# Decode step with paged attention: key pages transposed on VectorE in 32x32 blocks, scores in 32x32 tiles of TensorE

## The chip, the cores and the metric

The kernel runs on one core of one Trainium2 chip, in one launch. The metric is the time on the device in microseconds. Before the change three runs took 1260.12, 1259.9 and 1259.26 us (median 1259.9).

## The reference, cut to what matters

One layer of a decoder trunk, all in fp32, for 512 prompt tokens and for 8 sample sequences of 8 new tokens each, with the same weights. Model width is 1024.

```python
h = rms_norm(x) ; qkv = h @ w_in                      # 1024 x 3072, then rotary on q and k
# A) differential attention: 4 heads, two 64-wide components, values 128 wide
oa = (softmax(q1 k1^T) - lam * softmax(q2 k2^T)) v ; oa = rms_norm_per_head(oa) * (1 - lambda_init)
# B) dilated window attention: 8 heads x 64, union of (128,1), (512,4), (2048,16)
x += concat(oa, ob) @ w_out
x += (silu(h2 @ w_gate) * (h2 @ w_up)) @ w_down       # h2 = rms_norm(x), FF = 2816
y = rms_norm(x)
```

The sample sequences look back on 4096 past tokens. For A the keys and values lie in pages of 128 tokens x 512 numbers (256 KB), 32 per sequence, found through a page table. For B they are 2048 rows of 512 numbers per sequence, of which 10 blocks of 128 rows are read. So 336 blocks ("pages") of keys and 336 of values are loaded, 176 MB in all. New keys, values and the shifted windows are outputs as well.

## The kernel before, in words

**Slots.** Two sequences make an item. There are 8 items: 4 for A, of 8 quads each, and 4 for B, of 3 quads each, 44 quads in all (`KSLOTS`). A quad is 4 pages of each of the two sequences (2 of each in the last quad of a B item). The middle of the kernel is a loop over slots `t` and steps `i` = 0..7, written out in the same order on every engine. In slot t the keys of quad t are scored, and the values of quad t - 8 (`LAG`) are weighed. Slots 0 to 7 have keys only, 44 to 51 values only.

**Keys of a slot.** SP loads page (t, i) into `k_ring[i]` once the page that lay there has been read (L563). TensorE turns it with four 128x128 transposes into one of two PSUM banks `TB` (`turn_page`, L988). ACT (even pages, L1374) and VectorE (odd pages, L1686) copy the bank to `kt_sb`, which holds four pages, one half of a slot. After pages 0 to 3, and again after 4 to 7, `score_keys` (L1016) multiplies: for each of 4 heads f, 128 rows of contraction, 32 query rows and 512 keys, into 32 partitions of bank `S`. The query blocks `q_bd` are written by POOL (L741). At the end of the slot VectorE takes the scores out of `S` with mask and running maximum (`keep_scores`, L1711).

**Values of a slot.** Probabilities are transposed through bank `X` (L1028), copied by ACT (L1384) and multiplied with the value pages (L1049).

**Pieces.** Everything of the prompt is cut into 297 pieces that are strung between the steps: 192 of the projection (24 tiles of 8 pieces, each 6 matmuls, L833), 2 for the last transposes, 70 of prompt attention (32 units of 128 queries, two pieces a unit, and 3 units of run-out), 33 of the w_out product (8 tiles of 4, L964, and the last way back, L977). `upto(t, i)` says how many pieces are done by a step: 32 before slot 0, 5 a slot up to slot 6, some 5.3 a slot up to slot 43, and the 33 of w_out over slots 44 to 51. A unit's two score matmuls (L879) go to the banks `M[0]` and `M[1]`, rows 0 to 63 and 64 to 127 of the array; VectorE masks both (L1602). Outputs of prompt attention and transposed tokens use bank `Y`.

**Queues.** SP issues all loads in the order of the loop. Between the pages it puts the weight chunks (512 KB each), window shifts, at slot 44 the four blocks of x (L652 waits for the last unit of prompt attention), and at slot 46 the 4 MB load of w_out into `wo_sb` (L677), which the sample product L1142 needs. Behind the slots come L1142, the second norm, and the FFN (L1114).

Of the kernel before, what the change touches and what calls it, by code (L numbers as in the profile page):

```python
# [15 lines left out]
P = 128  # L16
# [168 lines left out]

def upto(t, i):
    if i < 0:
        t, i = t - 1, 7
    if t < 0:
        return 8 * PRE  # L190
    if t < 7:
        return 8 * PRE + 5 * t + -(-5 * (i + 1) // 8)
    if t < KSLOTS:
        a = 8 * PRE + 35
        return a + -(-(OUT - a) * (8 * (t - 7) + i + 1) // (8 * (KSLOTS - 7)))
    return min(PIECES, OUT + -(-(PIECES - OUT) * (8 * (t - KSLOTS) + i + 1) // (8 * LAG)))
# [19 lines left out]
def x_order():  # L216
    out = []
    for t in range(SLOTS):
        for i in range(8):
# [6 lines left out]
            for p in pieces(t, i):  # L226
                if ATTN <= p < OUT:
# [10 lines left out]
def y_order():  # L238
    out = []
    for p in range(ATTN):  # L240
        n, j = divmod(p, 8)
        if j == 5 and 0 < n < TILES and kind_of(n - 1):
            out.append(("t", n - 1))
        if (n, j) in GROUP_AT:
            out.append(("g", GROUP_AT[n, j]))
        if p == 8 * TILES:
            out.append(("t", TILES - 1))
        if p == 8 * TILES + 1:
            out.append(("g", 3))
    out += [("a", T) for T in range(KT)]  # L250
    return {what: k for k, what in enumerate(out)}


X_NO, Y_NO = x_order(), y_order()
# [44 lines left out]
def build(nc, ins, outs):  # L299
    from contextlib import ExitStack  # L300
    ctx = ExitStack()
    with ctx:
# [13 lines left out]
        small = at("small", [P, 184], region(768))  # L316
# [17 lines left out]
        o_lo = [at("o_lo0", [P, D], W0 + 31744, F32R), at("o_lo1", [P, D], W0 + 4096, F32R)]  # L334
# [7 lines left out]
        qT = at("qT", [P, KT, NT], Q0)  # L342
        kT = at("kT", [P, KT, NT], Q0 + 18432)
# [33 lines left out]
        y_prompt = at("y_prompt", [P, 2, SEQ], KS)  # L377
# [6 lines left out]
        pt_sb = at("pt_sb", [P, 2, 4, P], region(4096))  # L384
        ptm = at("ptm", [NS, P], region(512))
        q_bd = at("q_bd", [P, 2, 2, 4, 32], region(2048))
# [19 lines left out]
        g_max = small[:, 96:105]  # L406
# [42 lines left out]
        x_full, x_free, y_full, y_free = sem("x_full"), sem("x_free"), sem("y_full"), sem("y_free")  # L449
# [6 lines left out]
        qbd_zero, q_ready = sem("qbd_zero"), sem("q_ready")  # L456
        t_done, kt_act, kt_dve = sem("t_done"), sem("kt_act"), sem("kt_dve")
# [45 lines left out]
        def _(sp):  # L503
# [75 lines left out]
            def store_k(n):  # L579

                T = tile_of(n)
                sp.wait_ge(y_free, Y_NO["t", n] + 1)
# [4 lines left out]
            def store_group(g):  # L587

                s, keys = g // 2, g % 2 == 0
                sp.wait_ge(y_free, Y_NO["g", g] + 1)  # L590
# [18 lines left out]
            def main(p):  # L609
# [21 lines left out]
                if p == ATTN + 8:  # L631
                    sp.wait_ge(y_free, Y_NO["g", 3] + 1)
# [15 lines left out]
            for t in range(SLOTS):  # L648
                for i in range(8):
                    h, k = divmod(i, 4)  # L650
                    if has_k(t + 1) and k < pages_of(t + 1):
                        sp.wait_ge(t_done, PAGE_NO[t, i] + 1 if k < pages_of(t) else half_end(t, h))  # L652
                        load_page(True, t + 1, i)
                    for p in pieces(t, i):
                        main(p)
                    if k == 3 and has_v(t + 1) and t < KSLOTS:
                        q = t + 1 - LAG
                        if t == KSLOTS - 1:
                            sp.wait_ge(t_done, half_end(t, h))
# [63 lines left out]
        def _(pool):  # L723
# [7 lines left out]
            def fetch_q(it):  # L731

                if it >= 2:
# [1147 lines left out]
```

## Time and profile before

| | |
|---|---|
| median of 3 runs | 1259.9 us |
| the profiled execution | 1257.03 us |
| its span, first to last instruction | 1255.1 us |
| mean granted TensorE clock | 0.968 of full |
| busy: PE, DVE, ACT, POOL | 88%, 34%, 37%, 20% |
| DMA queue of the loads | 74.2% of 16 engines' span, 314 MB |
| last instruction of the keys' stage | 681.4 us |

The slots lie between 55.9 us (first copy of a page) and 785.1 us (start of L1142). Busy shares are means over the span; a stretch has its own limit, so the table by stretches is the view to read. A matmul's record lasts some 0.27 us although the next one starts much sooner, so records overlap, and one fp32 matmul of 32 columns of weights leaves two records.

### The profile page before, as it was taken

Reading aid. Unit: us, or ns where it says so; the run is one execution under the profiler, and the core shown is the slowest. Engines: PE = TensorE matmul, PEld = TensorE weight load, DVE = VectorE, ACT = ScalarE, POOL = GpSimd, SP = SyncE. Lnnn points to the kernel's source line nnn. Section 1 sums busy time; section 2 is a strip of 40 time slices with the busy share of each in tenths; the row PEclk is TensorE's granted clock in tenths of the full one; section 3 lists DMA queues with packets and bytes.
Section 4 is the critical chain, followed back from the end, with each engine's and each line's share of the span. In section 5 each row is a group of like instructions: output and inputs, shape, how many; then the busy total and the mean of one; then the engine's idle time right before and its main releaser. Section 6 shows DMA issues by size and latency. Waiting matters only on the chain.

```text
span 1255.1 us, 27090 instructions
## 1 busy us (share of the span) xinstructions
PE 1108.4 (88%) x10450; PEld 960.5 (77%) x10450; DVE 424.5 (34%) x839; ACT 467.4 (37%) x844; POOL 254.3 (20%) x138
## 2 busy tenths in 40 slices
PE   4888899989999998888888659699999999999994
PEld 4776678878777875555556547499999999999994
DVE  4334322343333236566564101523323232300002
ACT  5634443454544335565554202332222222211122
POOL 1311010101111000002001111133333333434340
PEclk8999999999999999999999879799999999999998
DMA  8578999999999999877566883657777666644422
GB/s 271 201 269 301 310 369 339 349 368 333 348 331 326 352 334 363 243 227 259 180 187 205 250 268 132 209 201 248 248 250 249 246 219 243 215 160 137 156 81 75
DMA packets 210932, 315.43 MB, mean 251 GB/s; under 512 B 14289, under 2 KB 118994, under 8 KB 209810
## 3 DMA queue, kind: packets, MB, share of 16 engines
q1 hardware_dynamic: 210834, 314.09, 74.2%
q8 instruction: 65, 1.06, 0.3%
q14 instruction: 33, 0.27, 0.1%
HBM read 306.96 MB, written 73.92 MB: 303 GB/s over the span
## 4 chain that ended last, share of the span: by engine, by line
PE 76%; DVE 7%; DMA 6%; ACT 5%; issue 5%; POOL 1%; SPq 1%; DVEq 0%; ACTq 0%; POOLq 0%
PE main_ps L1114 34%; PE main_ps L833 11%; PE main_ps L988 10%; PE so_ps L1016 7%; PE so_ps L1049 5%; DMA o_raw<-in_w_out 3%; DMA k_ring<-in_state_k_win 2%; PE main_ps L964 2%; PE main_ps L879 1%; DVE kt_sb L1686 1%; PE tr_ps L1028 1%; PE tr_ps L908 1%; DVE prob L1602 1%; DVE h_lo L1563 1%; PE tr_ps L889 1%
## 5 line engine op out<-in xcount | busy, mean ns | idle before, releaser
L796 POOL TENSOR_TENSOR c_lo<-c_raw,c_hi 128x1024 fp32r<-128x1024 f32 (+1 forms) x60 | 157.2, 2619 | 298.4 <-ACT c_hi L1446 298.4
L988 PE MATMUL main_ps<-ident,k_ring 128*128 128x128 f32 x1344 | 198.6, 279 | 5.9 <-DMA k_ring<-in_state_k_win 4.0
L1686 DVE COPY kt_sb<-main_ps 128x512 f32<-128x512 f32 x168 | 115.9, 690 | 254.7 <-PE main_ps L988 254.4
L1446 ACT ACTIVATE c_hi<-c_raw 128x1024 fp32r<-128x1024 f32 (+1 forms) x60 | 68.8, 1147 | 319.9 <-PE main_ps L1114 265.4
L1374 ACT ACTIVATE kt_sb<-main_ps 128x512 f32<-128x512 f32 x168 | 99.8, 594 | 229.4 <-PE main_ps L988 228.7
L988 PEld LDWEIGHTS main_ps<-ident,k_ring 128*128 128x128 f32 x1344 | 154.1, 142 | 36.3 <-issue 30.9
L1114 PE MATMUL main_ps<-h_hi,c_hi 128*128 128x288 f32 x704 | 151.7, 297 | 1.9 <-DVE h_lo L1563 1.9
L1114 PE MATMUL main_ps<-h_hi,c_lo 128*128 128x288 f32 x704 | 151.5, 297 | 0.0
L1114 PE MATMUL main_ps<-h_lo,c_hi 128*128 128x288 f32 x704 | 151.3, 297 | 0.0
L1016 PE MATMUL so_ps<-kt_sb,q_bd 128*32 128x512 f32 (+1 forms) x704 | 91.7, 590 | 46.9 <-DVE kt_sb L1686 23.9
L833 PE MATMUL main_ps<-h_hi,w_hi 128*128 128x288 f32 x384 | 128.4, 334 | 3.1 <-DVE h_lo L1563 1.9
L728 POOL TENSOR_TENSOR w_lo<-w_raw,w_hi 128x1024 fp32r<-128x1024 f32 x24 | 58.7, 2448 | 357.1 <-ACT w_hi L1215 357.0
L1114 PEld LDWEIGHTS main_ps<-h_hi,c_hi 128*128 128x128 f32 x704 | 114.1, 190 | 2.1 <-DVE h_lo L1563 2.1
L833 PE MATMUL main_ps<-h_hi,w_lo 128*128 128x288 f32 x384 | 114.3, 298 | 0.0
L833 PE MATMUL main_ps<-h_lo,w_hi 128*128 128x288 f32 x384 | 114.3, 298 | 0.0
L1114 PEld LDWEIGHTS main_ps<-h_hi,c_lo 128*128 128x128 f32 x704 | 113.9, 190 | 0.0
L1114 PEld LDWEIGHTS main_ps<-h_lo,c_hi 128*128 128x128 f32 x704 | 113.9, 190 | 0.0
L1049 PEld LDWEIGHTS so_ps<-v_ring,pt_sb 128*32 128x32 f32 x2464 | 73.1, 111 | 50.1 <-issue 38.1
L1049 PE MATMUL so_ps<-v_ring,pt_sb 128*32 128x128 f32 x2464 | 84.6, 276 | 10.0 <-ACT pt_sb L1384 10.0
L833 PEld LDWEIGHTS main_ps<-h_hi,w_hi 128*128 128x128 f32 x384 | 73.7, 192 | 3.8 <-DVE h_lo L1563 2.1
L1114 PE MATMUL main_ps<-a_hi,c_hi 128*128 128x288 f32 x352 | 75.8, 297 | 0.0
L1114 PE MATMUL main_ps<-a_hi,c_lo 128*128 128x288 f32 x352 | 75.5, 296 | 0.0
(159 smaller groups left out, 1522.3 us busy)
## 6 DMA issues: line engine op xcount, KB each, us to landing
k_ring<-in_cache_k_diff SPq DMA_DIRECT2D x256, 256.0 KB, 5.8
v_ring<-in_cache_v_diff SPq DMA_DIRECT2D x256, 256.0 KB, 5.3
out_k_win_sample<-in_state_k_win SPq DMA_DIRECT2D x32, 1020.0 KB, 7.3
out_v_win_sample<-in_state_v_win SPq DMA_DIRECT2D x32, 1020.0 KB, 7.9
k_ring<-in_state_k_win SPq DMA_DIRECT2D x80, 256.0 KB, 5.8
v_ring<-in_state_v_win SPq DMA_DIRECT2D x52, 256.0 KB, 5.3
w_raw<-in_w_in SPq DMA_DIRECT2D x24, 512.0 KB, 7.2
c_raw<-in_w_gate SPq DMA_DIRECT2D x22, 512.0 KB, 3.9
```

Of the source, the lines that this page charges most:

```text
L728: nc.gpsimd.tensor_tensor(w_lo[:, n % 2, :], w_raw[:, n % 2, :], w_hi[:, n % 2, :].bitcast(F32), ALU.subtract).then_inc(w_lo_done, 1)
L796: nc.gpsimd.tensor_tensor(c_lo[:, j, 0:width], c_raw[:, j, 0:width], c_hi[:, j, 0:width].bitcast(F32), ALU.subtract).then_inc(w_lo_done, 1)
L833: last = nc.tensor.matmul(M[c][:, 0:HALF], wt[:, n % 2, w], act[:, k, c * HALF:(c + 1) * HALF], start=k == 0 and at_first, stop=k == KT - ...
L879: last = nc.tensor.matmul(M[c][:, 0:n], qT[r, T, qb * P:(qb + 1) * P], kT[r, T, 0:n], start=True, stop=True)
L964: last = nc.tensor.matmul(M[m % 2], wt[m % 2][:, w], act[:, k, 0:SEQ], start=k == 0 and at_first, stop=k == KT - 1 and wt is o_lo)
L988: last = nc.tensor.transpose(TB[no % 2][:, f * P:(f + 1) * P], k_ring[:, i, f * P:(f + 1) * P], ident[:, :])
L1016: last = nc.tensor.matmul(S[32 * f:32 * f + 32, 0:n], q_bd[:, it % 2, h, f, :], kt_sb[:, f, 0:n], start=h == 0, stop=h == 1)
L1049: last = nc.tensor.matmul(O[32 * f:32 * f + 32, P * h:P * h + P], pt_sb[:, t % 2, k, 32 * f:32 * f + 32], values[:, 4 * h + k, f * P:(f + ...
L1114: last = nc.tensor.matmul(main_ps[:, 2 * bank + c, 0:HALF], wt[:, j, w], act[:, k0 + k, c * HALF:(c + 1) * HALF], start=start and k == 0 a ...
L1374: nc.scalar.activation(kt_sb[:, :, k * P:(k + 1) * P], TB[0].rearrange("p (f c) -> p f c", f=4), ACT.Copy)\
L1446: nc.scalar.activation(c_hi[:, j, 0:width], c_raw[:, j, 0:width], ACT.Copy).then_inc(w_hi_done, 1)
L1686: V.tensor_copy(kt_sb[:, :, k * P:(k + 1) * P], TB[1].rearrange("p (f c) -> p f c", f=4)).then_inc(kt_dve, 1)
```

## The change

Five things change together.

1. **Keys.** `turn_page` leaves TensorE. VectorE transposes each of the 8 pages of a slot in 32x32 blocks straight from `k_ring` to `kt_sb`; ACT copies no page any more. SP's next load into the ring and the start of the scores wait for VectorE (`kt_done`).
2. **Scores.** A block transpose leaves the feature blocks of a head on different row groups. So the scores are 4 rounds r of 4 row groups b and 4 heads f, each a 32x32 tile of the array on 128 keys. Row group b writes bank b of four banks `S`. `keep_scores` evacuates page by page from the four banks. The query blocks `q_blk` hold four shifted copies, written by ACT (`fetch_q`); POOL has no part in it.
3. **Banks.** Four banks go to `S`, so `Y` goes: transposed tokens share `X`, prompt attention's outputs use `M[1]`, and its two score matmuls take `M[0]` in turn. The w_out tiles are turned back in their own bank. `pt_sb` has one buffer instead of two.
4. **Shares.** The list `SHARE` replaces `upto`'s formula: 5 pieces in each of slots 0 to 7, 8 in slots 8 to 23, 5 in slots 24 to 37, 4 from slot 38. Prompt attention lies in slots 23 to 36 and the w_out product in slots 37 to 44.
5. **Loads.** x is loaded in slot 37, and `wo_sb` in four parts of 1 MB in slots 44 to 47.

```diff
+SHARE = [5] * 8 + [8] * 16
+SHARE = SHARE + [5] * 14
+SHARE = SHARE + [4] * 9 + [0] * (SLOTS - 47)
...
-    return min(PIECES, OUT + -(-(PIECES - OUT) * (8 * (t - KSLOTS) + i + 1) // (8 * LAG)))
+    return min(PIECES, 8 * PRE + sum(SHARE[:t]) + -(-SHARE[t] * (i + 1) // 8))
...
-        main_ps = psum("main_ps", 4)
-        tr_ps = psum("tr_ps", 2)
-        so_ps = psum("so_ps", 2)
-        M = [main_ps[:, 0, :], main_ps[:, 1, :]]
-        TB = [main_ps[:, 2, :], main_ps[:, 3, :]]
-        X, Y = tr_ps[:, 0, :], tr_ps[:, 1, :]
-        S, O = so_ps[:, 0, :], so_ps[:, 1, :]
+        ps = psum("ps", 8)
+        main_ps, tr_ps = ps[:, 0:4, :], ps[:, 4:6, :]
+        M = [ps[:, 0, :], ps[:, 1, :]]
+        S = ps[:, 2:6, :]
+        X, O = ps[:, 6, :], ps[:, 7, :]
...
-                        sp.wait_ge(t_done, PAGE_NO[t, i] + 1 if k < pages_of(t) else half_end(t, h))
+                        sp.wait_ge(kt_done, PAGE_NO[t, i] + 1 if k < pages_of(t) else half_end(t, h))
                         load_page(True, t + 1, i)
...
-                    if (t, i) == (KSLOTS, 0):
+                    if t == 37 and i % 2 == 1:
                         sp.wait_ge(pv_done, UNITS)
                         sp.wait_ge(v_stored, 16 * (2 + DB + 1))
-                        for blk in range(4):
-                            load_x(blk)
-                    if (t, i) == (KSLOTS + 2, 7):
+                        load_x(i // 2)
+                    if KSLOTS <= t < KSLOTS + 4 and i == 5:
                         sp.wait_ge(mix_lo, KT)
-                        sp.dma_start(wo_sb[:, :, :], w_out).then_inc(wo_in, 16)
+                        k2 = 2 * (t - KSLOTS)
+                        sp.dma_start(wo_sb[:, k2:k2 + 2, :], w_out[:, k2:k2 + 2, :]).then_inc(wo_in, 16)
...
-            def scores(u):
+            def scores(u, c):
...
-                for c in range(2):
-                    r = slice(64 * c, 64 * c + 64)
-                    last = nc.tensor.matmul(M[c][:, 0:n], qT[r, T, qb * P:(qb + 1) * P], kT[r, T, 0:n],
-                                            start=True, stop=True)
-                last.then_inc(scores_done, 1)
+                r = slice(64 * c, 64 * c + 64)
+                nc.tensor.matmul(M[0][:, 0:n], qT[r, T, qb * P:(qb + 1) * P], kT[r, T, 0:n],
+                                 start=True, stop=True).then_inc(scores_done, 1)
...
-            def turn_page(t, i):
-
-                no = PAGE_NO[t, i]
-                pe.wait_ge(k_landed[i], K_LANDS[t, i])
-                if no >= 2:
-                    pe.wait_ge(kt_dve if no % 2 else kt_act, no // 2)
-                for f in range(4):
-                    last = nc.tensor.transpose(TB[no % 2][:, f * P:(f + 1) * P], k_ring[:, i, f * P:(f + 1) * P], ident[:, :])
-                last.then_inc(t_done, 1)
...
-                for f in range(4):
-                    last = nc.tensor.matmul(S[32 * f:32 * f + 32, 0:n], q_bd[:, it % 2, h, f, :], kt_sb[:, f, 0:n],
-                                            start=h == 0, stop=h == 1)
+                for r in range(4):
+                    for b in range(4):
+                        quad = slice(32 * b, 32 * b + 32)
+                        for f in range(4):
+                            c = 32 * (4 * f + r)
+                            last = nc.tensor.matmul(S[32 * f:32 * f + 32, b, 0:32 * n], q_blk[quad, h, (r - b) % 4, f, :],
+                                                    kt_sb[quad, 0:n, c:c + 32],
+                                                    start=h == 0 and r == 0, stop=h == 1 and r == 3)
                 last.then_inc(scored if h else half_scored, 1)
...
+            def turn_page(t, i):
+
+                dve.wait_ge(k_landed[i], K_LANDS[t, i])
                 if i >= 4:
                     dve.wait_ge(half_scored, t + 1)
                 elif t:
                     dve.wait_ge(scored, t)
-                k = i % 4
-                V.tensor_copy(kt_sb[:, :, k * P:(k + 1) * P], TB[1].rearrange("p (f c) -> p f c", f=4)).then_inc(kt_dve, 1)
+                V.transpose(kt_sb[:, i % 4, :], k_ring[:, i, :]).then_inc(kt_done, 1)
...
+                for k in range(pages_of(t)):
+                    c = 512 * g + P * k
+                    mask = lw[:, c:c + P] if it >= 4 else zero.to_broadcast([P, P])
+                    col = 4 * g + k + (0 if it < 4 else 22)
+                    c = col0(it, g) + P * k
+                    last = V.tensor_tensor_reduce(out=s_sb[:, c:c + P].rearrange("p (b j) -> p b j", b=4),
+                                                  in0=S[:, :, 32 * k:32 * k + 32],
+                                                  in1=mask.rearrange("p (b j) -> p b j", b=4), scale=1.0, scalar=-3e38,
+                                                  op0=ALU.add, op1=ALU.max, accum_out=g_max[:, col:col + 1])
+                last.then_inc(s_evac, 1)
```

The rest follows from it: `mask_max` masks one half of a unit at a time, the rotary step writes prompt and sample parts with two additions instead of one and starts once both products can be made, and the split mix of the w_out product lies in the space of q and k (`mix_h`, `mix_l`).

## Rows read from the trace of the kernel before

**Rows 1.** The page: granted clock and DMA share in forty slices of 31.4 us.
```profile
PEclk8999999999999999999999879799999999999998
DMA  8578999999999999877566883657777666644422
```

**Rows 2.** Busy time by stretch: microseconds, busy (instructions), clock, DMA share, GB/s.
```profile
56.00:154.40 98.40, 83.64 (x648) 66.06 (x647) 39.45 (x64) 42.14 (x69) 14.07 (x13) 0.97 0.86 293
154.40:371.50 217.10, 202.46 (x2433) 170.90 (x2436) 72.88 (x133) 100.48 (x174) 27.58 (x19) 1.00 1.00 346
371.50:576.90 205.40, 181.70 (x2157) 137.46 (x2147) 100.61 (x271) 100.28 (x229) 12.39 (x17) 0.99 0.92 307
576.90:681.00 104.10, 84.18 (x954) 57.54 (x955) 53.98 (x163) 50.00 (x122) 12.10 (x11) 0.97 0.63 199
681.00:785.00 104.00, 76.09 (x754) 57.21 (x744) 18.97 (x47) 26.38 (x46) 16.94 (x7) 0.87 0.70 215
```

**Rows 3.** VectorE in order of time at four slot ends: start, length, operation.
```profile
154.37 0.69 DVE L1711 CUSTOM_DVE_ANT_0 s_sb<-so_ps,small 128x512 f32<-128x512 f32 x1 [1.27 <-PE so_ps L1016]
371.47 0.69 DVE L1711 CUSTOM_DVE_ANT_0 s_sb<-so_ps,small 128x512 f32<-128x512 f32 x1 [1.57 <-PE so_ps L1016]
576.87 0.36 DVE L1711 CUSTOM_DVE_ANT_0 s_sb<-so_ps,lw 128x256 f32<-128x256 f32 x1
681.02 0.42 DVE L1711 CUSTOM_DVE_ANT_0 s_sb<-so_ps,lw 128x256 f32<-128x256 f32 x1 [2.56 <-PE so_ps L1016]
```

**Rows 4.** Groups of instructions by shape: busy, mean ns, idle before and releaser.
```profile
L988 PE MATMUL main_ps<-ident,k_ring 128*128 128x128 f32 x1344 | 198.6, 279 | 5.9 <-DMA k_ring<-in_state_k_win 4.0 <-DVE kt_sb L1686 1.1 <-ACT kt_sb L1374 0.8
...
L1686 DVE COPY kt_sb<-main_ps 128x512 f32<-128x512 f32 x168 | 115.9, 690 | 254.7 <-PE main_ps L988 254.4
...
L1546 DVE SCALAR_TENSOR_TENSOR xn<-x,small,g_rows 128x1024 f32<-128x1024 f32 x4 | 5.1, 1285 | 1.0 <-PE tr_ps L817 0.6 <-PE main_ps L817 0.3
...
L1602 DVE CUSTOM_DVE_ANT_0 prob<-main_ps,p_mask 128x128 f32<-128x128 f32 x16 | 4.0, 288 | 5.2 <-PE main_ps L879 5.1
...
L1711 DVE DVE_READ_ACCUMULATOR2_ANT small<- 128x1 f32 x44 | 3.6, 83 | 0.0
L1619 DVE TENSOR_SCALAR prob<-prob,small 128x512 f32<-128x512 f32 x8 | 3.5, 484 | 0.1
```

**Rows 5.** L1686 alone, then L1711 alone, in the third and fourth stretch.
```profile
371.50:576.90 205.40, 35.82 (x52) 0.99 0.92 307
576.90:681.00 104.10, 13.71 (x20) 0.97 0.63 199
...
371.50:576.90 205.40, 9.52 (x29) 0.99 0.92 307
576.90:681.00 104.10, 3.50 (x12) 0.97 0.63 199
```

**Rows 6.** TensorE in order of time: start, length, operation, records.
```profile
302.80 1.08 PE L1049 MATMUL so_ps<-v_ring,pt_sb 128*32 128x128 f32 x32
...
304.23 0.38 PE L833 MATMUL main_ps<-h_hi,w_hi 128*128 128x288 f32 x1
...
305.10 0.60 PE L988 MATMUL main_ps<-ident,k_ring 128*128 128x128 f32 x4
...
515.49 0.43 PE L1000 MATMUL so_ps<-kT,q_bd 128*32 128x64 f32 x16
...
549.10 1.13 PE L879 MATMUL main_ps<-kT,qT 64*128 64x512 f32 x4
```

**Rows 7.** The chain that ended last, 640 to 812 us: start, length, what.
```profile
689.02 16.07 DMA o_raw<-in_w_out
...
724.28 23.93 DMA o_raw<-in_w_out
...
785.13 8.79 PE so_ps L1142 x32
```

**Rows 8.** DMA issues in the fifth stretch: count, size, us to landing.
```profile
wo_sb<-in_w_out SPq DMA_DIRECT2D x1, 4096.0 KB, 22.8
```

More of the change, by code:

```diff
@@ L226, in x_order @@
             for p in pieces(t, i):
+                n, j = divmod(p, 8)
+                if p < 8 * TILES and j == 5 and n and kind_of(n - 1):
+                    out.append(("t", n - 1))
+                if (n, j) in GROUP_AT:
+                    out.append(("g", GROUP_AT[n, j]))
+                if p == 8 * TILES:
+                    out.append(("t", TILES - 1))
+                if p == 8 * TILES + 1:
+                    out.append(("g", 3))
                 if ATTN <= p < OUT:
@@ L235, in x_order @@
     return {what: k for k, what in enumerate(out)}
[L238 to L254, printed above, removed]
+X_NO = x_order()
 EXP_NO = {what: k for k, what in enumerate(w for t in range(SLOTS) for i in range(8) for w in exps_at(t, i))}
@@ L405, in build @@
         rstd = small[:, 80:96]
-        g_max = small[:, 96:105]
+        g_max = small[:, 178:211]
         row_max = small[:, 105:106]
@@ L941, in main @@
                     u = a - 2
-                    if half == 0 and a < UNITS:
-                        scores(a)
+                    if a < UNITS:
+                        scores(a, half)
                     if 0 <= u < UNITS and (half == 0 or u // 4 >= 4):
@@ L962, in out_tile @@
                         pe.wait_ge(mix_lo, k + 1)
[L963 to L964 removed]
+                    for wt, act, at_first in ((o_hi, mix_h, True), (o_hi, mix_l, False), (o_lo, mix_h, False)):
+                        last = nc.tensor.matmul(M[m % 2], wt[m % 2][:, w], act[:, k, :],
                                                 start=k == 0 and at_first, stop=k == KT - 1 and wt is o_lo)
@@ L1138, in _ @@
             pe.wait_ge(s_evac, KSLOTS + ITEMS)
-            pe.wait_ge(wo_in, 16)
+            pe.wait_ge(wo_in, 16 * 4)
             for k in range(KT):
                 for h in range(2):
-                    last = nc.tensor.matmul(S[NS * h:NS * h + NS, :], oT_s[:, k, :], wo_sb[:, k, 512 * h:512 * h + 512],
+                    last = nc.tensor.matmul(O[NS * h:NS * h + NS, :], oT_s[:, k, :], wo_sb[:, k, 512 * h:512 * h + 512],
                                             start=k == 0, stop=k == KT - 1)
@@ L1320, in main @@
                         evac_weights(u, half)
-                    if half == 0 and a < UNITS:
+                    if half == 1 and a < UNITS:
                         expo(a)
@@ L1554, in add_sample_out @@
                     c = slice(512 * h, 512 * h + 512)
-                    last = V.tensor_tensor(x[0:NS, 4, c], x[0:NS, 4, c], S[NS * h:NS * h + NS, :], ALU.add)
+                    last = V.tensor_tensor(x[0:NS, 4, c], x[0:NS, 4, c], O[NS * h:NS * h + NS, :], ALU.add)
                 last.then_inc(xs_added, 1)
@@ L1649, in main @@
                     a, half = divmod(p - ATTN, 2)
-                    if half == 0 and a < UNITS:
-                        mask_max(a)
+                    if a < UNITS:
+                        mask_max(a, half)
                     if half == 1 and 1 <= a <= UNITS:
```

250 lines of the change are left out of this document (108 added, 142 removed).

## The prediction

> **What bounds the kernel now.** I read the page first, then a table of five stretches, then VectorE's order of time, the groups by shape, single TensorE records and the end of the chain of waits.
>
> The page shows the DMA engines at 9 tenths from about 125 to 530 us, and TensorE near 9 tenths there too [rows 1]. A slot is one step of the paged attention: 8 pages of keys and 8 of values (4 and 4 in four late slots). Its end is VectorE's evacuation of the scores, L1711: slot 7 ends at 155.1 us, slot 23 at 372.2, slot 36 at 577.2, slot 43 at 681.4 [rows 3]. The stretches of the table end there. The reader is to see four regimes [rows 2]:
> - slots 0 to 7 (keys only): 12.3 us each, DMA share 0.86, TensorE busy 85%;
> - slots 8 to 23: 13.6 us each at a DMA share of 1.00: the transfers set the pace, though TensorE is 93% busy;
> - slots 24 to 36 (205.4 us, share 0.92) and 37 to 43 (104.1 us, 0.63): TensorE first, projections and then prompt attention beside the pages;
> - 681 to 785 us: values only, and the w_out product of the prompt. DMA share 0.70, TensorE busy 76 of 104 us, clock 0.87. In the chain two w_out chunks take 16.07 and 23.93 us to land [rows 7]: they are issued on SP behind value pages, and the second just behind the 4 MB load of wo_sb (22.8 us) [rows 8].
> Behind 785.1 stand L1142, the second norm and the FFN, which the change leaves as they are but for names of banks.
>
> **What leaves TensorE, and what comes.** Per full slot 32 page transposes go: 198.6 us over 1344 [rows 4] is 0.148 us each at most, 4.7 us a slot. The scores were 8 matmuls of 512 columns (16 records), 4 tiles side by side. They become 128 matmuls of 128 columns in 32x32 tiles, which I count as 256 records, because the matmuls of L1049 make two each: 32 records for 16 of them in 1.08 us, the pipe's 0.27 us at the end included, so 27 ns a record [rows 6]. What a record costs when 16 tiles run side by side no row shows. One end: 27 ns, if only the four column tiles overlap: 7 us a slot. Other end: four times less, 1.8 us. L1000 has 16 records of 64 columns in 0.43 us, 14 ns each without the pipe's end, so issue is no floor at 27 ns; and L879 runs two row halves into two banks: four records of 512 columns in 1.13 us [rows 6]. By L1049 a record of 128 columns streams for 4 x 27 ns = 0.107 us, one of 512 for 0.43; less the 0.27 the four took twice that and not four times, so row tiles overlap when their banks differ. The new rows go to four banks. I take 1.0 us per half slot with the pipe's end. The Trainium skill speaks against this: "TensorEngine Tiling (Array Packing)", Instruction Overhead, puts some 60 cycles on every matmul, and "TensorE: Matmul & The Clock Gate", Part 1, has starts never nearer than about 25 ns. At 25 ns the scores would take 6.4 us a slot, which is nearly my dearer end. L1000's 14 ns [rows 6] disagrees with both, and the measurement decides.
>
> A projection piece (six matmuls) takes 0.87 us from 304.23 to the transposes at 305.10 [rows 6]. So slots 8 to 23 with 8 pieces need 7.0 + 2.0 + values 2.0 + some 1 for other transposes = 12 us of TensorE: below the DMA.
>
> **What comes onto VectorE.** Before, it copied 4 of the 8 pages of a slot (0.69 us each). Now it transposes all 8, SBUF to SBUF, 128x512. No row shows a transpose. Lower end 0.48 us (a one-source SBUF operation of that size, L1619); upper end 1.23 us (two passes, about the 1.285 us of 1024 elements of L1546) [rows 4]. I take 0.69, the copy of the same size: 5.5 us a slot. The skill's "VectorE: DVE Perf Modes", The three transpose paths, gives 311 ns for 128x128 bf16; less 128 elements and plus 512 at its 0.96 GHz, that is an estimate of 0.71 us, which would add 0.2 us a slot.
> The evacuation becomes four operations of 128x128: 0.288 each (L1602 of that shape) and 0.083 for each read of the maximum [rows 4]: 1.5 us instead of 0.77.
> The rest of VectorE: slots 0 to 7 have 39.45 - 32x0.69 - 8x0.77 = 11.2 us, 1.4 a slot. Slots 8 to 23 have 72.88 - 44.2 - 12.3 = 16.4 for 10.7 tiles, 1.5 a tile, now one tile a slot; a split addition adds 0.2 to a tile. Prompt attention: 100.61 + 53.98 less 49.5 for copies and 13.0 for scores [rows 2, 5] = 92 us, once over slots 24 to 43, now in 13 slots: 7.1 each.
> New waits: kt_sb has one buffer, so the first transpose of a half waits for the scores of the half before. What is queued behind it on VectorE (rope, masks, normalising) waits too, and SP's next key load and TensorE's next prompt scores wait for those. The evacuation already idles 1.27 us for TensorE [rows 3]. I take 1.3 us twice a slot, and 0.9 where attention pieces lie between page and scores.
>
> **The sum by stretches.**
> - Slots 0 to 7: 5.5 + 1.5 + 1.6 + 2.6 = 11.2 us; the DMA needs 0.86 x 98.4 / 8 = 10.6. Total 90 instead of 98.4: -8.
> - Slots 8 to 23: VectorE's chain is 5.5 + 1.5 + 1.7 + 2.6 = 11.3, under the DMA. The DMA now carries 16 weight tiles instead of 10 here, 3.1 MB at 346 GB/s = 9, and some 2 for stores that come earlier: 228 instead of 217: +11. Freeing TensorE gains nothing here.
> - Slots 24 to 36: 5.5 + 1.5 + 7.1 + 0.2 + 1.8 = 16.1; 12 full slots and one short one (12.6) make 206 instead of 205.4. The DMA needs 0.92 x 205 - 11 = 178. TensorE's bound turns into VectorE's.
> - Slots 37 to 43: now with the w_out product in place of attention. VectorE 9.6, TensorE about 11 a slot; DMA 0.63 x 104.1 = 66, plus 6 w_out chunks (9) and x (6) = 81. With gaps 90 instead of 104: -14.
> - Values only: 0.70 x 104 = 73 of DMA, less 15 moved = 58; wo_sb comes in four parts that do not stand in front of anything late. 62 instead of 104: -42. This is the largest term. The cover of the w_out tiles is gone there: if TensorE idles between value slots its clock falls to its lower level (it was 0.50 in the waits of this stretch's slices, 0.87 on average); +2 for L1142 and the norm.
> ACT loses 168 copies and gets the query blocks (24 small copies an item) in place of POOL; it was busy 100 of 217 us at most per stretch, so nothing. The one bank X for both old transposing banks: its users are spaced by pieces, nothing, bounded in the rivals. SP waits at slot 37 for the last attention unit before it loads x; that unit ends in slot 36: nothing.
> Sum: -8 + 11 + 1 - 14 - 42 + 2 = -50 us (L1142 at 735). The profiled execution took 1257.0 us (span 1255.1), so 1207; the median of the runs is 2.9 above it: 1210.
>
> **Rivals.**
> - A, slower: the transpose is two passes, 1.23 us. VectorE gets 4.3 us a slot more. Slots 0 to 7 become 15.5 (+34), 8 to 23 become 15.6 instead of 14.25 (+22), 24 to 36 +54, 37 to 43 +1: +111, time 1321. It turns slower from about 0.93 us on. For it: no row shows VectorE turning 4-byte blocks. Against: its simple operations grow by 0.13 to 0.14 us for 128 elements (0.288 at 128, 0.69 at 512) whatever they do [rows 4].
> - B, slower: row tiles don't overlap: 27 ns a record, +2.5 us a half. +41 (slots 0 to 7), +34 (16.4 instead of 14.25), +62, +13: 1360. Against it: L879 and L1000. The clock page's 25 ns, as 6.4 us a slot by the same steps, would give an estimate of 1330. It turns slower from 1.8 us per half on.
> - C, faster still: waits of a half are hidden and slots 24 to 36 fall to the DMA's 178 (-28), slots 0 to 7 to 85 (-5): 1177. For it: those scores come while VectorE has masks to do.
> - D, hardly any change: prompt scores use one bank M[0] by turns, so each of 64 halves of units waits for the mask of the one before, and VectorE for a matmul of up to 0.7 us; if none of it is hidden, 45 us: 1255. Against: between two such pieces VectorE has 1.6 transposes, 1.1 us.
>
> **How the numbers follow.** Forecast 0.57, C 0.11, D 0.13, A 0.10, B 0.09. A measurement tells 0.2% (2.5 us) from no change. Faster: 0.57 + 0.11 + half of D = 0.75; same 0.03; slower 0.22. The likeliest's own range is 1180 to 1240; to hold 8 in 10 I take 1165 to 1270.
>
> **What would show it.** The transposes at 0.65 to 0.75 us; 128 records of half a slot's scores in about 1.1 us; slots 8 to 23 at 14.2 us each with DMA share 1.00; slots 24 to 36 with VectorE above 85% busy; last key slot at 667 to 675 us; L1142 near 735. Wrong if the last key slot ends after 700, or if the stretch from it to L1142 stays above 80 us: then the tail was not the loads' queue.

## The result: slower by a sixth, and the profile after

The changed kernel takes 1468.9 us (median of 4 runs, 1461.4 to 1473.2) against 1259.6 us (1256.9 to 1260.1) of the kernel before: ratio 1.166 [1.161, 1.171]. Forecast were 1210 us, with a range to 1270. The prediction is wrong in sign. The profiled span is 1471.4 us against 1255.1.

First two rows of the page after, clock and DMA share in forty slices of 36.8 us; they answer to [rows 1].
```profile
PEclk8888898898896675577767799656999999999998
DMA  8578887968777564554455786865567776754431
```
The DMA engines reach 9 in a single slice, and TensorE's clock stands at 5 to 7 tenths from about 440 to 850 us; slots 24 to 36 had 9 before.

The stretches after, at the ends of slots 7, 23, 36, 43 and at the start of the samples' product (L1102, L1142 before); columns as in [rows 2].
```profile
56.00:166.50 110.50, 79.51 (x2319) 68.51 (x2317) 59.27 (x149) 31.91 (x74) 11.82 (x5) 0.83 0.77 253
166.50:471.20 304.70, 252.32 (x6015) 216.67 (x6017) 120.36 (x326) 91.77 (x198) 33.09 (x14) 0.86 0.81 266
471.20:794.90 323.70, 253.50 (x4776) 161.99 (x4772) 160.07 (x482) 104.86 (x287) 16.30 (x10) 0.68 0.52 170
794.90:921.20 126.30, 97.70 (x2524) 74.79 (x2516) 41.86 (x119) 30.18 (x80) 14.18 (x6) 0.89 0.75 234
921.20:1002.10 80.90, 43.47 (x540) 22.61 (x532) 10.01 (x34) 11.41 (x23) 0.00 (x0) 0.62 0.67 218
```
To compare them, an error of my reading has to be mended. The third row of [rows 3] is the end of slot 37; slot 36 of the kernel before ended here (VectorE in order of time, then the two stretches of before with this end):
```profile
559.80 0.69 DVE L1711 CUSTOM_DVE_ANT_0 s_sb<-so_ps,lw 128x512 f32<-128x512 f32 x1 [1.27 <-PE so_ps L1016]
...
372.20:560.50 188.30, 166.70 (x1965) 127.27 (x1961) 86.00 (x237) 91.35 (x205) 9.51 (x15) 0.99 0.93 311
560.50:681.50 121.00, 98.99 (x1141) 67.72 (x1140) 68.36 (x197) 59.43 (x146) 14.98 (x13) 0.97 0.66 209
```
That moves 17 us between two measured stages and leaves their sum as it was (309.3 us for 309.5). It does not leave the forecast as it was. For slots 24 to 36 it now says 18 us more than before, not 1 more. The 90 us for slots 37 to 43 rest on a DMA need read from six slots (0.63 x 104.1 = 66); by the row above it is 0.66 x 121.0 = 80, and with the 15 moved there 95. Stage by stage, in us of the profiled executions (half_rounds is the first experiment below):

| stage | before | forecast | after | half_rounds |
|---|---|---|---|---|
| to the end of slot 7 | 155.1 | 147 | 166.5 | 150.9 |
| slots 8 to 23 | 217.1 | 228 | 304.7 | 228.5 |
| slots 24 to 36 | 188.3 | 206 | 323.7 | 268.4 |
| slots 37 to 43 | 121.0 | 90 | 126.3 | 120.9 |
| values only | 103.6 | 62 | 80.9 | 83.2 |
| L1102 and the FFN | 470.0 | 472 | 469.3 | 461.7 |

So 88 and 135 of the 216 us more were lost in slots 8 to 23 and 24 to 36, and the tail gained 23.

From slot 24 on the rows do not hold the same work, though, and my working missed that. I had prompt attention over slots 24 to 43 of the kernel before. In its trace the attention scores L879 start at 462.8 us, at the end of slot 30: slots 24 to 30 hold projection, and attention takes slots 31 to 43, 214.9 us at a clock of 0.98. After, attention lies in slots 24 to 36 (L852 from 451.6 us), 323.7 us at 0.68, and the w_out product has come in from the tail. So a like comparison for attention is 109 us more, if only roughly (four short slots there, one here); slots 24 to 43 together took 309.3 us before, 450.0 after and 389.3 in half_rounds.

VectorE's page transposes and TensorE's key scores after, as groups (columns as in [rows 4]; records overlap, so the mean says how long one is under way, not what it costs):
```profile
L1650 DVE STREAM_TRANSPOSE kt_sb<-k_ring 128x512 f32<-128x512 f32 x336 | 217.4, 686 | 166.0 <-PE ps L977 162.5 <-DMA k_ring<-in_state_k_win 3.2
L977 PE MATMUL ps<-kt_sb,q_blk 32*32 32x128 f32 (+1 forms) x11264 | 194.0, 313 | 87.9 <-DVE kt_sb L1650 59.3 <-issue 19.8 <-ACT q_blk L1333 8.2
```
A transpose costs 686 ns (forecast 690): rival A is out. But VectorE idles 162.5 us ahead of them for the scores, and TensorE 59.3 us ahead of the scores for them.

What the scores cost, TensorE in order of time: a half slot at the full clock, its first 0.2 us alone, a half at the lower level, and a half of the four-page slots.
```profile
247.20 1.91 PE L977 MATMUL ps<-kt_sb,q_blk 32*32 32x128 f32 x128
...
247.20 0.47 PE L977 MATMUL ps<-kt_sb,q_blk 32*32 32x128 f32 x27
...
612.11 2.82 PE L977 MATMUL ps<-kt_sb,q_blk 32*32 32x128 f32 x128
...
801.92 1.48 PE L977 MATMUL ps<-kt_sb,q_blk 32*32 32x64 f32 x128
```
A half takes 1.91 us, not 1.0: above the 1.8 at which rival B, by its own working, turns the change slower. 27 records start within the first 0.2 us, 7 ns apart, which is what I had assumed for all 128. Behind the 32nd record, that is the 16th matmul, the starts are wider apart: one matmul (two records) every 16.5 ns, and with 128 columns every 17th matmul stands alone. From the first start to the last a half takes 1.64 us, 13 ns a record. The 16.5 ns are the same with 64 columns (the last row) and at the lower clock (the third), so neither the stream of columns nor the array's clock sets them. The pauses do change: a matmul that stands alone takes 109 ns to its second record, 213 at the lower clock and 57 with 64 columns. Halving the columns saves only 0.43 of 1.91 us: most of the cost is in the number of records.

The first 32 pairs of weight load and matmul are 64 instructions. The Trainium skill ("TensorE: Matmul & The Clock Gate", the table at its head) gives TensorE's queue a depth of 64; the trace agrees with a queue filled while the longer matmuls before it ran (at 247.20 us) or while the engine waited. It does not prove it: in 16 matmuls each of the 16 tiles is also used once, and the pause at every 17th may be the re-use of a tile. No run separates the two. The Trainium skill's other rule, some 60 cycles a matmul ("TensorEngine Tiling (Array Packing)", Instruction Overhead), would be an estimate of 25 ns; for single records the trace disagrees, with 7 ns at first and a mean of 13 over the half. Counted by the program's matmuls, of two records each, the mean over the half is 25.6 ns (1.64 us for 64), but it is made up of 7, 16.5 and pauses, and it moves with the columns and the clock.

### The profile page after: what moved, and what is told of

Its sections match the earlier page's. It is cut to its first block, busy times and chain, and to the rows that moved or that the text cites. A ratio compares the mean times of both kernels' runs of the same rounds, so it can differ in the third digit from the quotient of the medians.

```text
span 1471.4 us, 45615 instructions
## 1 busy us (share of the span) xinstructions
PE 1207.0 (82%) x19666; PEld 1016.1 (69%) x19666; DVE 535.2 (36%) x1271; ACT 417.7 (28%) x868; POOL 246.7 (17%) x106
## 4 chain that ended last, share of the span: by engine, by line
PE 70%; DVE 9%; issue 8%; DMA 6%; ACT 4%; SPq 2%; POOL 0%; DVEq 0%; ACTq 0%
PE ps L1074 29%; PE ps L977 12%; PE ps L807 10%; PE ps L1011 7%; DVE kt_sb L1650 4%; PE ps L852 4%; DMA v_ring<-in_state_v_win 3%; SPq L571 2%; PE ps L937 2%; PE ps L880 2%; PE ps L990 1%; DMA k_ring<-in_state_v_win 1%; PE ps L861 1%; DMA k_ring<-in_state_k_win 1%; ACT q_blk L1333 1%
## 5 line engine op out<-in xcount | busy, mean ns | idle before, releaser
L1650 DVE STREAM_TRANSPOSE kt_sb<-k_ring 128x512 f32<-128x512 f32 x336 | 217.4, 686 | 166.0 <-PE ps L977 162.5
L977 PE MATMUL ps<-kt_sb,q_blk 32*32 32x128 f32 (+1 forms) x11264 | 194.0, 313 | 87.9 <-DVE kt_sb L1650 59.3
L977 PEld LDWEIGHTS ps<-kt_sb,q_blk 32*32 32x32 f32 x11264 | 149.2, 113 | 128.7 <-DVE kt_sb L1650 70.6
L1011 PE MATMUL ps<-v_ring,pt_sb 128*32 128x128 f32 x2464 | 117.8, 330 | 60.1 <-issue 46.1
L1074 PE MATMUL ps<-h_hi,c_hi 128*128 128x288 f32 x704 | 151.8, 297 | 1.9 <-DVE h_lo L1529 1.9
L1074 PE MATMUL ps<-h_lo,c_hi 128*128 128x288 f32 x704 | 151.4, 297 | 0.0
L1074 PE MATMUL ps<-h_hi,c_lo 128*128 128x288 f32 x704 | 151.3, 297 | 0.0
L807 PE MATMUL ps<-h_hi,w_hi 128*128 128x288 f32 x384 | 134.4, 350 | 9.5 <-issue 6.9
L807 PE MATMUL ps<-h_lo,w_hi 128*128 128x288 f32 x384 | 124.9, 325 | 2.9 <-issue 2.9
L807 PE MATMUL ps<-h_hi,w_lo 128*128 128x288 f32 x384 | 124.6, 324 | 0.0
```

The costliest lines, as they stand in the source:

```text
L807: last = nc.tensor.matmul(M[c][:, 0:HALF], wt[:, n % 2, w], act[:, k, c * HALF:(c + 1) * HALF], start=k == 0 and at_first, stop=k == KT - ...
L977: last = nc.tensor.matmul(S[32 * f:32 * f + 32, b, 0:32 * n], q_blk[quad, h, (r - b) % 4, f, :], kt_sb[quad, 0:n, c:c + 32], start=h == 0 ...
L1011: last = nc.tensor.matmul(O[32 * f:32 * f + 32, P * h:P * h + P], pt_sb[:, k, 32 * f:32 * f + 32], values[:, 4 * h + k, f * P:(f + 1) * P] ...
L1074: last = nc.tensor.matmul(main_ps[:, 2 * bank + c, 0:HALF], wt[:, j, w], act[:, k0 + k, c * HALF:(c + 1) * HALF], start=start and k == 0 a ...
L1650: V.transpose(kt_sb[:, i % 4, :], k_ring[:, i, :]).then_inc(kt_done, 1)
```

## Experiments

Two theories. T1: the price is the issue of small records, 256 a slot, with what follows from TensorE being late. T2 (rival): the price is the coupling, VectorE and TensorE waiting for each other through one kt_sb and one bank, or the new shares. The expectations on record call T1 theory S (supply), and the two parts of T2 theory L (lockstep) and theory D (the shares).

**half_rounds: half the contraction.** 

> The changed kernel with only rounds 0 and 1 of the four rounds of score matmuls (64 records instead of 128 per half slot's... 32 matmuls instead of 64); the other half of each score's contraction is left out. Theory S (supply): the many small matmuls are the cost, at 15 ns a record once TensorE's queue is empty, plus gaps of TensorE without any wait (68 us in the changed kernel) while its program is fetched, plus the clock that falls behind them. It expects some 0.9 us less per half slot (-80), half of the gaps gone (-35) and some clock back: 1300 to 1350 us. Theory L (lockstep): VectorE's page transposes stand behind masks and rope that wait for TensorE, and the other way round; record cost matters little. It expects 1420 or more.


```
-                for r in range(4):
+                for r in range(2):
...
-                                                    start=h == 0 and r == 0, stop=h == 1 and r == 3)
+                                                    start=h == 0 and r == 0, stop=h == 1 and r == 1)
```
1311.5 us, ratio to before 1.043 [1.033, 1.053]; 157 us less than after. Its half slot of scores, then its second and third stretch:
```profile
183.63 1.07 PE L977 MATMUL ps<-kt_sb,q_blk 32*32 32x128 f32 x64
...
150.90:379.40 228.50, 202.44 (x3975) 169.87 (x3977) 128.05 (x326) 91.26 (x198) 33.30 (x14) 0.92 1.02 354
379.40:647.80 268.40, 220.22 (x3117) 133.86 (x3109) 160.54 (x480) 104.99 (x287) 16.32 (x10) 0.68 0.63 203
```
With scores at the price that I had forecast (1.07 us), slots 8 to 23 take 228.5 us at a DMA share of 1.02: the forecast's 228. So the size of the scores is what sank that term. That it hits 228 exactly is in part luck: with the transposes earlier (half_turns_first, below) the same stage takes 217.1 us at 370 GB/s, where the sum had counted with 346. Slots 24 to 36 are not mended: 268 us at a clock of 0.68. The first stage speaks for T1; in the other something more is at work.

**quarter_rounds: a quarter of it** (`range(1)`, stop at r == 0). 

> The changed kernel with one of the four rounds of score matmuls (16 matmuls, 32 records a half slot); three quarters of each score's contraction are left out. Half the rounds gave 1311 us, with 0.80 us a half slot for 64 records and 1 us of gaps without a wait. Theory S in its plain form (cost by record) expects another 0.5 us a half slot at most, and slots 8 to 23 already at the pace of the DMA: 1270 to 1300 us. If the whole loss scaled with the number of small matmuls, the time would fall by a further 80 to about 1230. What is left above before is then the lockstep of VectorE and TensorE, not the scores.


1304.2 us, 1.036 [1.032, 1.041]: 7 us below half, with overlapping intervals, and just above the 1270 to 1300 of the plain theory. Once the scores are this short, their number is worth little or nothing.

**f_outside: the loops over banks and column tiles exchanged**, so that neighbouring records go to other row tiles. 

> The changed kernel with the two inner loops of the scores exchanged: the row groups change from one matmul to the next and the heads only every fourth; the same work. If the 15 ns a record come from how the tiles of the array follow each other, a half slot's 128 records take clearly more or less than 1.91 us, and the time moves by 20 us or more. If TensorE's supply of instructions sets them (theory S), 1.9 us again and the time within 15 us of 1469.


```
-                    for b in range(4):
-                        quad = slice(32 * b, 32 * b + 32)
-                        for f in range(4):
+                    for f in range(4):
+                        for b in range(4):
+                            quad = slice(32 * b, 32 * b + 32)
```
1452.1 us, 1.154 [1.147, 1.161]. The half slot:
```profile
202.99 1.90 PE L977 MATMUL ps<-kt_sb,q_blk 32*32 32x128 f32 x128
```
1.90 us for 1.91: whether neighbours differ in the row tile or in the column tile does not matter. Rival B's cause, row tiles that don't overlap at all, would have made some 3.5 us in either order (27 ns a record), and falls; its size is nearest all the same. The time is 17 us below after, between the 15 and the 20 of the two expectations; the lower clock up to slot 43 lasts 273 us here and 358 in after, and I have no cause for that.

**few_long: half_rounds with TensorE time put back as few, long matmuls.** 

> half_rounds (two of four rounds of score matmuls left out) with sixteen long matmuls a slot added: 128 rows, 32 columns of weights, 384 moving columns, 32 records, written to columns of bank S that nobody reads. By the 27 ns a record of 128 columns they take some 2.6 us a slot, a little more than the 1.7 us that the left-out rounds took. So TensorE's time is at least the changed kernel's and its records are 160 a slot instead of 256. If TensorE's time is all that counts, the whole 157 us come back: 1450 or more. If the gaps without a wait (68 us in the changed kernel, 1 in half_rounds) come from the amount of program and count by themselves, they stay under 15 us and the time lies between 1370 and 1420.


```
+                for e in range(4 if h == 0 else 0):
+                    for f in range(4):
+                        nc.tensor.matmul(S[32 * f:32 * f + 32, 0, P:4 * P], q_blk[:, h, e, f, :], kt_sb[:, 0, P:4 * P],
+                                         start=True, stop=True)
```
1400.4 us, 1.114 [1.107, 1.121]. The group added, and the second and third stretch:
```profile
L974 PE MATMUL ps<-kt_sb,q_blk 128*32 128x384 f32 x1408 | 145.0, 560 | 42.8 <-DVE kt_sb L1654 36.8 <-ACT q_blk L1337 5.7
...
170.80:424.30 253.50, 235.15 (x4486) 178.17 (x4489) 120.15 (x324) 91.23 (x198) 33.16 (x14) 0.98 0.94 313
424.30:718.90 294.60, 240.04 (x3520) 133.52 (x3516) 159.67 (x480) 104.97 (x287) 16.33 (x10) 0.79 0.57 188
```
It costs 89 us over half_rounds, of the 157 between that and after, though the added group alone is busy for 145.0 us; 68 us are missing. TensorE's records of after have 38 gaps up to slot 43, most of 1.5 to 4 us, ahead of an instruction that waits for nothing, 68 us together; half_rounds has 2 (1 us), few_long has 1 (0.5 us), before has none. One of them, TensorE in order of time after, then the row of the instruction fetches' queue on the pages of after, before and few_long (packets, MB, share):
```profile
255.34 0.64 PE L1011 MATMUL ps<-v_ring,pt_sb 128*32 128x128 f32 x15
259.12 1.27 PE L1011 MATMUL ps<-v_ring,pt_sb 128*32 128x128 f32 x17 [3.14 <-issue]
```
```profile
q8 instruction: 135, 2.21, 0.6%
```
```profile
q8 instruction: 65, 1.06, 0.3%
```
```profile
q8 instruction: 102, 1.67, 0.5%
```
A packet of 16 KB lies at 256.5 us, in this gap. Of the 24 gaps over 1.5 us, 19 have such a packet in them or in the 0.5 us ahead, and of the 14 shorter ones none (the packets are those of all engines). The gaps come with density: the five kernels with 256 records a slot (after, f_outside, turns_first, old_shares, turns_old_shares) have 38 to 49 gaps, 68 to 93 us in all, and those with 128 or 160 at most 7 (5 us). The program's packets are twice as many (135 for 65). Shown are the gaps, their absence with fewer records, and the packets beside them; that the fetch is their cause is inferred. That the missing 68 us equal the gaps' 68 is no proof either: few_long also stands for only 191 us at the lower clock.

**turns_first: VectorE transposes all pages of a half at its first step.** 

> The changed kernel with VectorE turning all four pages of a half at its first step, ahead of the masks and the rotary work of that half. Theory L expects 60 us or more off (1400 or less), since the scores no longer wait for transposes queued behind masks. Theory S expects 1455 to 1480: TensorE's own work sets the pace.


```
-                    if has_k(t) and i % 4 < pages_of(t):
-                        turn_page(t, i)
+                    if has_k(t) and i % 4 == 0:
+                        for k in range(pages_of(t)):
+                            turn_page(t, i + k)
```
1439.3 us, 1.144 [1.125, 1.164]: about 30 us less than after, but the two runs lie 20 us apart and the interval touches that of after. It is neither theory L's 1400 nor theory S's 1455.

**old_shares: the old shares of the pieces, x loaded at slot 44.** 

> The changed kernel with the old distribution of pieces (5.3 a slot up to slot 43, w_out over slots 44 to 51, x loaded in slot 44). Theory S: TensorE is the bound in nearly every key slot, so moving its work between them changes little; the w_out product back in the tail costs 20 to 50: 1470 to 1520 us. Theory D (the shares did it): 8 pieces a slot and attention packed into 13 slots are what hurt; it expects under 1400. Theory L: between, about 1430, since fewer masks stand between the pages of a slot.


```
-    return min(PIECES, 8 * PRE + sum(SHARE[:t]) + -(-SHARE[t] * (i + 1) // 8))
+    if t < 7:
+        return 8 * PRE + 5 * t + -(-5 * (i + 1) // 8)
...
```
1437.2 us, 1.143 [1.133, 1.152]: 32 us less than after, near theory L's 1430. So the new shares are part of the loss, and not the main part.

**turns_old_shares: both.** 

> The changed kernel, all of its computation kept, with both remedies together: VectorE turns the pages of a half first, and the pieces have their old shares. Alone they gave 1439 and 1437 us. If they act on different waits they add up: 1400 to 1415. If both only relieve the same lockstep in prompt attention, the two together give 1425 or more. Theory S expects the gaps without a wait to stay at 70 us or more either way, and the time far above 1256.


1426.8 us, 1.137 [1.127, 1.146]: 42 us less, not 62. The likely reason is that both spread the work that one engine has ready while the other is late, and so share one saving; the intervals of the three runs overlap, so that is argued and not shown. Four fifths of the loss stay, and the gaps without a wait are 93 us, as theory S had it (70 or more).

**half_turns_first: half_rounds with turns first.** 

> half_rounds with VectorE turning all pages of a half at its first step. With the supply of TensorE relieved, what is left above before (55 us) lies in slots 24 to 36, 268 us against 188. Theory L says that transposes queued behind masks make it: slots 24 to 36 fall to 240 or less, time 1285 or less. If it is the clock and the single bank for prompt scores instead, the order changes little: 1300 to 1320.


1282.9 us, 1.021 [1.015, 1.027]. Its third stretch:
```profile
360.00:615.90 255.90, 210.42 (x3119) 129.31 (x3109) 159.28 (x482) 104.97 (x287) 14.99 (x10) 0.72 0.65 214
```
The time meets theory L's 1285, but the stage does not fall to its 240: even with short scores and early transposes the attention stage takes 256 us, at a clock of 0.72. Another 19 us come off ahead of it (slots 8 to 23 take 217.1 us).

**one_bank_before: the kernel before, prompt scores by turns in one bank.** 

> The kernel before, with one part of the change alone: the two score matmuls of a prompt unit use bank M[0] in turn, each waiting for the mask of the one before, and the exponentials move to the second half of a unit. Theory L expects 30 to 60 us more than before (1290 to 1320). Theory S expects at most 10 more, since TensorE has other work there.


```
-                for c in range(2):
-                    r = slice(64 * c, 64 * c + 64)
-                    last = nc.tensor.matmul(M[c][:, 0:n], qT[r, T, qb * P:(qb + 1) * P], kT[r, T, 0:n],
-                                            start=True, stop=True)
-                last.then_inc(scores_done, 1)
+                r = slice(64 * c, 64 * c + 64)
+                nc.tensor.matmul(M[0][:, 0:n], qT[r, T, qb * P:(qb + 1) * P], kT[r, T, 0:n],
+                                 start=True, stop=True).then_inc(scores_done, 1)
```
1281.3 us, 1.019 [1.010, 1.028]. Its third stretch:
```profile
372.20:577.70 205.50, 185.30 (x1955) 135.02 (x1951) 86.78 (x235) 90.27 (x200) 9.51 (x15) 0.96 0.85 286
```
17 us in this stretch, 24 in all, less than theory L's 30 and more than theory S's 10: half of the 45 that rival D gave it, and not the nothing of the sum.

**shares_before: the kernel before with 5 pieces a slot to slot 7, then 8, attention from slot 24.** 

> The kernel before with one part of the change alone: 5 pieces a slot in slots 0 to 7, 8 in slots 8 to 23 (so the projection ends there), the attention pieces over slots 24 to 43; w_out as before. TensorE was 93% busy in slots 8 to 23: 43 more pieces there cost 37 us, and later slots give most of it back. Theory D (the uneven shares hurt by themselves) expects 1285 or more; theory S expects 1250 to 1275.


```
+    if t < 8:
+        return 8 * PRE + 5 * t + -(-5 * (i + 1) // 8)
+    if t < 24:
+        return 8 * PRE + 40 + 8 * (t - 8) + i + 1
```
1276.4 us, 1.014 [1.010, 1.019], just above theory S's 1275 and short of theory D's 1285. Its slots 8 to 23 against 217.1 us before:
```profile
157.10:405.40 248.30, 236.52 (x2699) 203.27 (x2698) 79.22 (x158) 115.75 (x214) 35.27 (x25) 1.00 0.95 315
```
With the page transposes still on TensorE the uneven shares make TensorE the bound (busy 95%). They presuppose a TensorE that is relieved, which in after it is not.

**wo_parts_before: the kernel before, wo_sb loaded in four parts.** 

> The kernel before with the 4 MB load of w_out cut into four parts of 1 MB, in slots 47 to 50, in place of one load in slot 46. In the chain before, a w_out chunk of the prompt product stands 23.9 us behind that load. If the loads' queue is what makes the stretch from slot 43 to L1142 long (as the prediction had it), it falls by 12 to 20 us: 1240 to 1248. If something else is late next there, within 4 us of before.


```
-                    if (t, i) == (KSLOTS + 2, 7):
+                    if KSLOTS + 3 <= t < KSLOTS + 7 and i == 5:
                         sp.wait_ge(mix_lo, KT)
-                        sp.dma_start(wo_sb[:, :, :], w_out).then_inc(wo_in, 16)
+                        k2 = 2 * (t - KSLOTS - 3)
+                        sp.dma_start(wo_sb[:, k2:k2 + 2, :], w_out[:, k2:k2 + 2, :]).then_inc(wo_in, 16)
```
1247.3 us, 0.992 [0.990, 0.994]: 0.8% faster than the kernel before. Its last stretch, and the loads of w_out in its chain of waits (start, length, what):
```profile
678.90:773.70 94.80, 74.82 (x738) 55.84 (x726) 18.70 (x46) 25.77 (x45) 16.93 (x7) 0.93 0.78 240
```
```profile
688.05 15.98 DMA o_raw<-in_w_out
...
722.53 11.47 DMA o_raw<-in_w_out
...
743.28 11.81 DMA o_raw<-in_w_out
```
The chunk that took 23.93 us behind the 4 MB load [rows 7] takes 11.47. That part of the reasoning on the tail holds, and is worth 9 us in the stretch.

**tail_before: the same, with x's four blocks at four steps of slot 44.** 

> The kernel before with w_out's load in four parts in slots 47 to 50 (which took 12 us off) and the four blocks of x loaded one by one over slot 44 instead of all at its start. The chain of wo_parts_before still shows 16.0 us for a w_out chunk behind the x blocks. If these are one more jam of the loads' queue, another 4 to 10 us go: 1238 to 1243 us. If x is late next at the first addition, 1247 to 1252.


1247.7 us, 0.992 [0.989, 0.995]: no further gain.

## Why the prediction was wrong

**The step that failed: "I take 1.0 us per half slot with the pipe's end."** It measured 1.91, and 2.82 at the lower clock. I had read from L1000 and L1049 that issue is no floor and from L879 that row tiles overlap [rows 6]. That issue allows 14 ns for 16 records and that tiles overlap is so; but L1000's run of 16 records ends before the 32nd, behind which the run of 128 gets slower. Sixteen records cannot show what 128 cost one after another. Twice 0.84 us (1.91 less half_rounds' 1.07) in 44 slots are 74 us; the gaps without a wait, 67 more than in half_rounds, come on top: 141 of the 157 us between half_rounds and after. Counted from start to start of the records up to slot 43, with the lower clock in it, the scores take 188 us in after and 98 in half_rounds; these 90 and the 67 make the 157. That is an addition and not a proof, since the waits and the clock moved as well.

**Slots 0 to 7** (+11 instead of -8): half_rounds has 4 us less than before. The transposes cost what I said; that the waits per half, taken at 1.3 us, grew with the scores is argued from that, not shown alone.

**Slots 8 to 23** (+88 instead of +11): TensorE, counted from start to start of its records from 165 to 473 us, spent 123 us on pieces, 65 on scores, 42 on values and 36 in gaps without a wait, and waited 17; with its other work that is 19.2 us a slot, 15.9 without gaps and waits, against my 12. The scores are 4.0 a slot for my 2.0, the pieces 7.7 for 7.0, the values 2.6 for 2.0. "Below the DMA" was wrong, and the DMA share fell to 0.81.

**Slots 24 to 36** (206 forecast, 324 measured): "TensorE's bound turns into VectorE's" was wrong. VectorE is busy 160 of 324 us (49%, where above 85% was to show it), TensorE 254, at a clock of 0.68. Neither is the bound: they take turns. TensorE, then VectorE, in order of time after, and three rows of the waits of this stretch (total us, times, longest):
```profile
612.11 2.82 PE L977 MATMUL ps<-kt_sb,q_blk 32*32 32x128 f32 x128
614.86 1.94 PE L1011 MATMUL ps<-v_ring,pt_sb 128*32 128x128 f32 x32
616.72 0.70 PE L852 MATMUL ps<-kT,qT 64*128 64x256 f32 x2
...
617.94 0.70 PE L852 MATMUL ps<-kT,qT 64*128 64x256 f32 x2
```
```profile
615.04 0.71 DVE L1650 STREAM_TRANSPOSE kt_sb<-k_ring 128x512 f32<-128x512 f32 x1 [1.65 <-PE ps L977]
617.45 0.42 DVE L1568 CUSTOM_DVE_ANT_0 prob<-ps,p_mask 128x256 f32<-128x256 f32 x1 [1.71 <-PE ps L852]
...
617.80 1.75 DVE L1627 RECIPROCAL sub_r<-sub_r 128x256 f32<-128x256 f32 x1
619.47 1.24 DVE L1650 STREAM_TRANSPOSE kt_sb<-k_ring 128x512 f32<-128x512 f32 x2
...
622.80 0.70 DVE L1650 STREAM_TRANSPOSE kt_sb<-k_ring 128x512 f32<-128x512 f32 x1
```
```profile
DVE prob L1568 <- PE ps L852: 51.0, 35, 4.9
...
DVE s_sb L1677 <- PE ps L977: 36.0, 13, 4.3
DVE kt_sb L1650 <- PE ps L977: 28.0, 11, 4.8
...
PE ps L977 <- DVE kt_sb L1650: 23.6, 12, 3.8
```
VectorE transposes one page when the old scores are read (615.04), stands in its queue before a mask whose scores TensorE makes only after the values (1.71 us), does a reciprocal of prompt attention (1.75 us), turns the next pages at 619.47 and the last at 622.80; only then do TensorE's next scores start, at 623.56. Each order is fixed, so a delay of the one is handed to the other and back. My sum added waits of 0.9 us to VectorE's work, as if TensorE were always ready. The experiments bound the parts: one bank alone is +17 us here in the kernel before, scores at my price still leave 268, early transposes take 12 off that. The rest of the 80 us between 268 and the 188 of before is not separated. Part of it is no loss but work that moved in: against the 214.9 us of attention in the kernel before, 268 is 54 more. The old shares were not run with short scores.

**The clock.** The granted clock was at its lower level (1.2 of 2.4 GHz) for 358 us up to slot 43, against 17 before, and there a half's scores take 2.82 us instead of 1.91. TensorE was idle before it fell: in the gap shown above it idles up to 259.12 us, and the clock is at its lower level from 258.3 to 265.1. That a slower TensorE makes VectorE wait longer, and so feeds the next fall, is argued. I had a clock term for the tail alone (2 us). How much of the 135 us it is stays open: in few_long the time at the lower level up to slot 43 fell from 268 (half_rounds) to 191 us while TensorE's work rose, and slots 24 to 36 grew by only 26 us for added matmuls that are busy for 48.6 us there. So a better clock gave something back, but how much of it is the clock alone can't be read off.

**Slots 37 to 43** (90 forecast, 126 measured; half_rounds 121): the DMA share is 0.75, so the transfers did not fill it, but they need 0.75 x 126.3 = 95 us, more than the whole forecast, which the misread end of slot 36 had made too small. The clock is 0.89. I ran nothing that separates the other 31 us.

**The tail** (62 forecast, 80.9 measured, 103.6 before): the load queue's part is right in sign. The chain after, in the last stretch (start, length, what), is value pages landing one after another; no w_out chunk is in it:
```profile
924.24 16.75 DMA v_ring<-in_state_v_win
...
954.66 18.61 DMA k_ring<-in_state_v_win
...
984.11 14.05 DMA v_ring<-in_state_v_win
```
At a share of 0.67 the transfers need 54 us, near my 58; what I left out is the latency of loads that are issued only when a page's buffer is free. By my own sign (above 80 us: then the tail was not the loads' queue) this is a miss by 1 us. wo_parts_before settles it better: the queue behind the 4 MB load is worth 9 us, not the 42 of the sum. The gain had nothing to set against 240 us lost ahead of it.

**Rivals.** A fell (686 ns). B was nearest in size and gave 1360, by a cause that the 1.91 us refute (it needs 3.5 a half). C and D asked the right question on waits of a half and the one bank, D with twice the price. None held a chain of two engines that slow each other, and the range ended 200 us too low.

In the FFN part half_rounds took 462 us, all other kernels in the table 469 to 470; this is not explained.

## What to carry to other kernels

Before work goes from one wide matmul to many small tiles, find the price of a record in a run as long as the new one: a short burst looked about twice as cheap here. Where two engines with fixed orders feed each other several times a slot through single buffers, add their chains instead of taking the larger; a stage can lose half its time with neither engine full. Separable parts of a change deserve a trial of their own: the split load of wo_sb gains 0.8% in the kernel before, and was hidden in a change that lost 17%.

## Hardware behaviour that I had not expected

- Pairs of 32x32 weight load and matmul records start 7 ns apart for the first 32. Then two start every 16.5 ns, at either clock and with 128 or 64 columns, with 128 columns also with a pause at every 17th matmul. It is the same whether neighbours share a row tile or a column tile (1.91 and 1.90 us for 128).
- With 256 such records a slot there are 38 gaps up to slot 43, most of 1.5 to 4 us, with nothing waited for, 68 us in all; with 128 a slot, 2 (1 us).
- VectorE transposes 128x512 of fp32 in 32x32 blocks in 686 ns, as long as its copy of that size (690 ns, [rows 4]).
- The mean granted clock was 0.68 over 324 us in which TensorE was busy 78% of the time; before it was 0.99 at 89%.
